# A third of the 4 MB expert-weight transfers issued from ScalarE's queue instead of SyncE's

## What is computed

```python
def expert_block(args):
    xb, e = args
    hgu = xb @ w_gate_up[e] + b_gate_up[e]
    h_gate, h_up = jnp.split(hgu, 2, axis=-1)
    h_gate = jnp.minimum(h_gate, SWIGLU_LIMIT)
    h_up = jnp.clip(h_up, -SWIGLU_LIMIT, SWIGLU_LIMIT)
    act = h_gate * jax.nn.sigmoid(SWIGLU_ALPHA * h_gate) * (h_up + 1.0)
    return act @ w_down[e] + b_down[e]
```

## Time and profile before

| What | Value |
|---|---|
| median of three runs | 1316.84 us |
| the profiled execution's own time | 1317.12 us |
| its span, first to last instruction | 1315.4 us |
| PE busy | 1257.4 us (96%) |
| ACT busy | 291.6 us (22%) |
| DVE busy | 574.1 us (44%) |
| DMA engines, share of the span in SP's queue (q1) | 86.8% |
| read from HBM | 465.89 MB |
| mean granted TensorE clock | 0.997 |

### The profile page before, as it was taken

How to read it: one execution, slowest core, us unless ns; L and a number is a source line. 1 busy time by engine, 2 the same in 40 slices (tenths; PEclk the granted TensorE clock), 3 DMA queues, 4 the chain that set the end, 5 groups by cost and what they waited for, 6 DMA issues and landing times.

```text
span 1315.4 us, 21204 instructions
## 1 busy us (share of the span) xinstructions
PE 1257.4 (96%) x8579; PEld 716.9 (55%) x8579; DVE 574.1 (44%) x1109; ACT 291.6 (22%) x510; POOL 15.1 (1%) x38
## 2 busy tenths in 40 slices
PE   8999999999999999998999999999999989999997
PEld 8999889999983343333333333334333333343332
DVE  6898899987646232322232222223222222222231
ACT  5453444445451111110110011001100110011111
POOL 2000000000000000000000000000000000000000
PEclk9999999999999999999999999999999999999999
DMA  9744453457788999999999999999999999999995
GB/s 319 241 161 139 137 172 128 152 169 228 272 356 328 420 430 430 430 430 428 432 431 432 432 432 433 432 431 430 430 430 431 432 432 431 432 431 425 428 428 221
DMA packets 77901, 467.48 MB, mean 355 GB/s; under 512 B 4391, under 2 KB 62295, under 8 KB 63303
## 3 DMA queue, kind: packets, MB, share of 16 engines
q1 hardware_dynamic: 77863, 466.95, 86.8%
HBM read 465.89 MB, written 1.05 MB: 355 GB/s over the span
## 4 chain that ended last, share of the span: by engine, by line
PE 65%; DMA 32%; DVE 2%; issue 1%; ACT 0%; DVEq 0%; SPq 0%; ACTq 0%
PE pb L825 18%; PE pb L581 18%; PE pb L852 10%; DMA work<-in_w_gate_up 7%; DMA work<-in_w_down 7%; DMA late_w<-in_w_gate_up 5%; DMA split_w<-in_w_gate_up 5%; DMA late_w<-in_w_down 4%; DMA split_w<-in_w_down 4%; PE pb L882 3%; PE pb L740 2%; PE pb L771 2%; PE pb L666 1%; PE pb L668 1%; PE pb L667 1%; PE pb L545 1%
## 5 line engine op out<-in xcount | busy, mean ns | idle before, releaser
L1663 DVE TENSOR_SCALAR work<-pb 64x512 f32<-64x512 f32 x64 | 43.7, 683 | 527.0 <-PE pb L832 525.8
L825 PE MATMUL pb<-work,ubuf 128*64 128x512 f32 x992 | 220.3, 597 | 19.8 <-DMA work<-in_w_gate_up 19.8
L581 PE MATMUL pb<-parts,whi 128*128 128x272 f32 (+1 forms) x1280 | 174.6, 287 | 0.1
L581 PEld LDWEIGHTS pb<-parts,whi 128*128 128x128 f32 x1280 | 163.1, 189 | 3.8 <-issue 3.4
L825 PEld LDWEIGHTS pb<-work,ubuf 128*64 128x64 f32 x992 | 74.3, 138 | 152.6 <-issue 152.4
L1215 DVE TENSOR_TENSOR wlo<-work,whi 128x1024 fp32r<-128x1024 f32 x104 | 126.4, 1222 | 34.7 <-ACT whi L984 34.4
L825 PE MATMUL pb<-late_w,ubuf 128*64 128x512 f32 x576 | 127.0, 593 | 9.2 <-DMA late_w<-in_w_gate_up 9.2
L984 ACT ACTIVATE whi<-work 128x1024 fp32r<-128x1024 f32 x104 | 109.9, 1060 | 112.8 <-PE pb L581 87.4
L852 PE MATMUL pb<-work,ubuf 128*64 128x512 f32 x576 | 131.2, 597 | 2.7 <-DMA work<-in_w_down 1.2
L825 PE MATMUL pb<-split_w,ubuf 128*64 128x512 f32 x472 | 104.1, 593 | 10.0 <-DMA split_w<-in_w_gate_up 9.6
L1150 ACT ACTIVATE work<-work 64x512 f32<-64x512 f32 x64 | 39.9, 624 | 281.7 <-DVE work L1663 281.7
(11 more groups left out here) (249 smaller groups left out, 1242.6 us busy)
## 6 DMA issues: line engine op xcount, KB each, us to landing
work<-in_w_gate_up SPq DMA_DIRECT2D x28, 4096.0 KB, 30.8
split_w<-in_w_gate_up SPq DMA_DIRECT2D x14, 4096.0 KB, 30.8
late_w<-in_w_gate_up SPq DMA_DIRECT2D x13, 4096.0 KB, 30.8
work<-in_w_down SPq DMA_DIRECT2D x12, 4096.0 KB, 29.0
work<-in_w_in SPq DMA_DIRECT2D x39, 1024.0 KB, 5.1
late_w<-in_w_down SPq DMA_DIRECT2D x7, 4096.0 KB, 29.0
split_w<-in_w_down SPq DMA_DIRECT2D x7, 4096.0 KB, 29.0
work<-in_w_down SPq DMA_DIRECT2D x11, 2048.0 KB, 18.5
```

The costliest lines, as they stand in the source:

```text
L581: ins = pe.matmul(pb[:, bank + j, 0:TALL - t0], w[:, x, k * UNIT + j * P:k * UNIT + (j + 1) * P], of[:, c * KC // 2 + k, t0:TALL], start=( ...
L825: ins = pe.matmul(pb[u * SLOTS:(u + 1) * SLOTS, bank, :], xT[:, 2 * i + k, :], w[:, k, u * HID:(u + 1) * HID], start=(i == 0 and k == 0), ...
L1663: dve.tensor_scalar(hg, pb[0:SLOTS, 4 + s, :], LIMIT, None, ALU.min).then_inc(min_rdy, 1)
```

## The change

ScalarE issues A of block b+2 directly behind the weighing of block b, for b = 1 to 25, that is numbers 10, 13, ..., 82: 25 of the 85 transfers. It does so in its own DMA queue, with no wait beyond that of the weighing, which covers the same count of `w_used`. SP leaves these numbers out and issues the other 60 as before. For the place of a transfer to be a constant, ScalarE's loop over blocks is written out by four: block 0 alone, six trips of blocks 4g+1 to 4g+4, block 25, blocks 26 and 27, and a loop over the `rounds` further blocks, for which ScalarE reads one more value.

```diff
             with sp.Fori(0, trips) as g:
                 for i in range(8, 20):
+                    if i % 3 == 1:
+                        continue
                     sp.wait_ge(w_used, 4 * LOADS * g + used(i - 4))
                     four(i, 4 * g)
             for i in range(8 + 12 * trips, fours):
+                if i % 3 == 1 and i < fours - 1:
+                    continue
                 sp.wait_ge(w_used, used(i - 4))
                 four(i, 0)
...
             sc.wait_ge(table_done, 4)
+            rounds = sc.value_load(nblocks[0:1, 0:1], min_val=NE - 1 - FIXED, max_val=MAXB - 2 - FIXED)
             last = sc.value_load(nblocks[0:1, 1:2], min_val=NE - 1, max_val=MAXB - 2)
...
             sigmoid(1)
-            with sc.Fori(0, last) as b:
+            def block(b):
 
                 sc.activation(stat[:, 20:21], mhalf[:, :], ACT.Sigmoid)
...
                 weigh(b, LOADS * b + 16)
+
+            def gate_up_four(b, j):
+
+                s = (3 * j + 7) % 4
+                sc.dma_start(place_at(4 * s, 4), expert_src(b + 2, w_gu, 1)).then_inc(e_in[s], 16)
+
+            block(0)
+            with sc.Fori(0, 6) as g:
+                for j in range(4):
+                    block(4 * g + (1 + j))
+                    gate_up_four(4 * g + (1 + j), 1 + j)
+            block(25)
+            gate_up_four(25, 25)
+            for b in range(26, FIXED):
+                block(b)
+            with sc.Fori(0, rounds) as i:
+                block(i + FIXED)
```

## The result

The changed kernel takes 1322.93 us (median of 7 runs, 1321.44 to 1326.35) against 1316.79 us of the kernel before (7 runs, 1315.76 to 1317.4): the medians lie 6.1 us apart. The ratio on record is 1.0054, with a 95% interval of 1.0045 to 1.0062, that is 5.9 to 8.2 us slower; it is not the quotient of the two medians. The profiled execution took 1322.38 us, its span is 1320.6 us.

What follows compares the result with a forecast made beforehand. The prediction took the full DMA engines (432 GB/s) to bound the stage, with PE limiting the blocks after it. It added only 7.57 us of C work at the stage's end to 1316.84 us: 1324.4 us, range 1316.5 to 1330 us.

Steps and rivals of the forecast that it cites:

- the main case: Whole kernel: A lands earlier, C comes last, the stage keeps its pace; 1322.7 to 1324.7 us, chance 0.55.
- What bounds it: Stage from 617.59 us: DMA engines full at 432 GB/s, 29.15 us per block, PE waiting mostly for A.
- What ACT adds, nothing: ACT, each block: issue and longer code hide in 9.27 us of idle time; A starts up to a microsecond later.
- Turns between the queues: Stage: with equal turns between two queues, A lands 21.1 us after issue instead of 30.8; pace stays the same.
- The waits move to C: Stage: PE's 2.5 us of waiting per block moves from L825 (A) to L852 (C), without cost inside the stage.
- The price of 7.57 us at the end: Stage end: after its last wait PE still has number 81's C work before 82, running 7.57 us later.
- the same moment, about 1173 us: Stage end: the last wait, now for number 81, ends when the wait for 82 did, the same four transfers having moved.
- The clock: Behind the last wait: the clock fall costing 1.7 us was left as is; without it, 1.7 us less.
- No cover behind: After the stage: numbers 83, 84 and the pairs arrive in time, PE limits the remaining blocks, nothing recovers 7.57 us.
- order kept: Rival, stage: engines serve both queues in order of issue, so nothing changes; 1316.8 us, chance 0.12.
- a change of the rate either way: Rivals, stage: rate up 0.9%, 1320.1 us (0.11); down, 1328.7 us (0.07); beyond the rows, 1314.8 us at 2% (0.10).
- uneven turns: Rival, stage: SP's queue gets two thirds, PE waits for A again, number 82 lands late; 1330 us, chance 0.05.

Runs made afterwards that it cites:

- e3: Changed kernel with ScalarE's loop still written out by four and reading the extra value but issuing nothing, SP issuing all 85 transfers: 1315.77 us, ratio 0.9996.
- e2: Changed kernel with ScalarE issuing only number 82 and SP the other 24 moved transfers: 1321.75 us, ratio 1.0047 to the kernel before.
- e7: Changed kernel with ScalarE issuing only numbers 10 to 43 (12 of the 25), SP all later ones: 1316.32 us, ratio 1.0001 to the kernel before.
- e8: Kernel before, all 85 transfers on SP, those around 400 to 440 us cut into finer pieces: 1314.30 us, ratio 0.9984.
- e1: Changed kernel with number 82 given back to SP, 24 of the 25 staying with ScalarE: 1319.27 us, ratio 1.0027 to the kernel before.
- e6: Changed kernel with numbers 79 and 82 given back to SP, the other 23 staying with ScalarE: 1317.71 us, ratio 1.0012 to the kernel before.
- e4: Kernel before with numbers 82 and 84 issued by SP as two 2 MB halves, TensorE waiting for each half: 1317.25 us, ratio 1.0011.

## Why the prediction was right

Forecast 1324.4 us, measured 1322.93 us; slower was forecast with 0.78, and the main case holds. Step by step:

- **What bounds it**: right. The rate stayed 432 GB/s with two queues and with one; number 84 landed at 1192.45 us after and 1192.31 us before.
- **What ACT adds, nothing**: right; e3 shows it for the longer code. ScalarE's issue took 0.34 us, ahead of some 7 us of idle time, and the weighing began 0.15 to 0.16 us ahead of it (0.01 us at the last of the 25), not up to a microsecond, as here in ACT's timeline after:

```profile
684.31 0.69 ACT L1171 ACTIVATE ubuf<-pb,stat 128x512 f32<-128x512 f32 x1 [4.42 <-PE pb L856]
684.46 0.34 ACTq L1187 DMA_DIRECT2D work<-in_w_gate_up  x1
684.89 0.19 ACT L1176 ACTIVATE stat<-mhalf 128x1 f32<-128x1 f32 x1
692.21 0.63 ACT L1155 ACTIVATE work<-work 64x512 f32<-64x512 f32 x1 [7.12 <-DVE work L1685]
```

- **Turns between the queues**: right in kind. An A lands 23.3 us after issue (the median), not 30.8 and not the 21.1 worked out. By the prediction's own sum that is an estimated 9.72 / (23.3 - 1.7) = 45% of the engines for ScalarE's queue while both held work. The Trainium skill's page "DMA: Bandwidth & Descriptors" says in "Issuing engines are not separate DMA queues" that transfers issued by different engines run on the same 16 DMA engines and interleave; the trace agrees, with 432 GB/s for both queues together. The same page of the Trainium skill says in "Queues, rings and completion order" that each of these engines takes turns between the queues it has work for; the trace agrees, with e2's landings, where 82 went past 81.
- **The waits move to C**: right, but not 2.5 us in each block. They come in 14 of the blocks, from 1.0 to 5.0 us, and the blocks between have none.
- **The price of 7.57 us at the end**: right mechanism, and 7.57 us lie within the measured 5.9 to 8.2 us; the medians are 6.1 us apart. The trace shows one term that was off. The C itself took 1179.42 - 1171.81 = 7.61 us. But "the same moment, about 1173 us" was wrong: 81 landed 2.5 us before 82, not behind it, so the last wait ended 1.2 us earlier, and TensorE began on 82 6.4 us later than before, not 7.57.
- **The clock**, left as it was: it fell in the profile of before behind the wait for 82 (0.57 in the mean from 1174 to 1178 us, much of it thus at the level of 1.2 GHz) and not in the profile after, behind 1.89 us of waiting (before 2.02). From the start on 82 to the residual's matmuls TensorE took 26.73 us after, against 28.47 us before with L825's 8.79 us in it; the residual's row before was:

```profile
1201.52 3.70 PE L874 MATMUL pb<-hx,ident 128*128 128x512 f32 x8
```

So of 6.4 us at 82 only 4.6 us are left at 1206.15 us and at the last engine instruction (1315.61 us, against 1310.98 before); the spans end 5.2 us apart. This fall belongs to the one execution of before that was profiled, not to the change: e3, e7 and e8, with SP's order at the end, took 7.09 us for the same group. The profiled executions also start the experts at different times: block 0's gathering (L771 before) begins between 406.89 us (e1) and 408.64 us (e6). Reckoned from there (408.28 us before, 407.10 in e3, 408.33 after), the span ends after 907.1 us before, 906.1 us in e3 and 912.3 us in the changed kernel: 6.2 us later than in e3, close to the 6.1 us of the medians.

- **No cover behind**: right for the changed kernel, which waits for no pair. But "limited by PE, as now" was only half of it: with SP's order the pairs land hardly earlier than TensorE wants them, as e3's wait of 0.16 us and e4 show.

The rivals: order kept is refuted by the landings; a change of the rate either way by 432 GB/s; uneven turns by the missing waits for an A.

## What to carry to other kernels

Here a bounded ring of buffers was full and the DMA engines were busy all the time, at 432 GB/s with one issuing queue and with two. The second queue changed only the order in which the transfers landed, and each transfer that landed earlier than it was wanted made others, wanted sooner, land later. Another kernel that is bound like this can be expected to do the same, which no run here tests. Inside the stage it cost nothing (e7), since the stream sets the pace; the price fell due where the stage ends, as the work that is still to be done behind the last wait. A consumer that is faster than the stream by 2.5 us per block worked off a lag of 7.6 us in about three blocks. What helped was to let the stream start earlier: cutting the first transfers finer, so that each piece goes as its part of a buffer comes free, made the kernel 2.1 us faster by the medians. And compare two profiled executions only from a common mark: here they differ by a microsecond or more ahead of the stage and by a clock fall at its end, as much as some of the effects looked for.

## What the runs showed of the hardware

The granted clock fell much more often in the changed kernel: 0.986 in the mean of the span against 0.997. Behind six of its eight waits of 3.42 to 5.00 us the first eight matmuls of a C took 3.24 to 3.68 us in place of 1.94 (behind the other two 2.40 and 1.94); one such stretch, from the profile after (the third column from the end is the clock, 0.50 there, the level of 1.2 GHz), and the wait before it in PE's timeline:

```profile
706.70:710.50 3.80, 3.75 (x9) 0.91 (x9) 0.00 (x0) 0.00 (x0) 0.00 (x0) 0.50 0.96 414
```

```profile
706.75 3.68 PE L856 MATMUL pb<-late_w,ubuf 128*64 128x512 f32 x8 [3.42 <-DMA late_w<-in_w_down]
...
881.68 1.94 PE L856 MATMUL pb<-work,ubuf 128*64 128x512 f32 x8 [3.52 <-DMA work<-in_w_down]
```

It does not follow from the wait's length alone: behind 3.42 us at 706.75 us the clock fell, behind 3.52 us at 881.68 us it did not, and in the kernel before it fell behind 2.02 us at 1173.05 us but not behind the same wait at 706.76 us. In the stage these falls cost nothing, as e7 shows, whose mean clock was 0.987 to 0.994 in its runs (0.994 to 0.998 before) at the time of the kernel before. What decides whether one comes at the end of the stage, where it costs up to 1.7 us, was not tried. Why the changed kernel's runs lie up to 4.9 us apart, those of before 1.6 us, is open: its fastest run (1321.44 us) and its slowest (1326.35 us) have the same mean clock, 0.982.
